# Transposing the branch inputs and merged rows on VectorE in 32x32 squares instead of on TensorE

## What is computed

```python
y_a = diff_attention(...) * silu(da_z)
y_b = mlstm(...) * silu(ml_z)
y_c = dsa_attention(...) * silu(dsa_z)
g = sigmoid(gates.reshape(b, s, 3, D_MODEL))
mixed = (g[:, :, 0] * (y_a @ w_branch[0])
         + g[:, :, 1] * (y_b @ w_branch[1])
         + g[:, :, 2] * (y_c @ w_branch[2]))
out = mixed @ w_out
x = x + rmsnorm(out, post_norm_g)
```

## Time and profile before

| | value |
|---|---|
| median of 3 runs | 1119.33 us |
| the profiled execution | 1117.77 us |
| its span in the profile | 1116.0 us |
| PE busy | 1100.3 us, 99% |
| DVE busy | 659.3 us, 59% |
| ACT busy | 540.7 us, 48% |
| POOL busy | 63.0 us, 6% |
| DMA, mean | 184 GB/s |
| mean granted clock of PE | 0.998 |

### The profile page before, as it was taken

How to read it: one execution, slowest core, us unless ns; L and a number is a source line. 1 busy time by engine, 2 the same in 40 slices (tenths; PEclk the granted TensorE clock), 3 DMA queues, 4 the chain that set the end, 5 groups by cost and what they waited for, 6 DMA issues and landing times.

```text
span 1116.0 us, 15365 instructions
## 1 busy us (share of the span) xinstructions
PE 1100.3 (99%) x5208; PEld 913.3 (82%) x5208; DVE 659.3 (59%) x928; ACT 540.7 (48%) x722; POOL 63.0 (6%) x111
## 2 busy tenths in 40 slices
PE   7999999999999999999999999999999999999997
PEld 6798888888887888889887778888888888888886
DVE  4555444665556676667866566665565545556445
ACT  4655444545555454544445444454444444435442
POOL 1000000100100011220310000000000000000000
PEclk9999999999999999999999999999999999999999
DMA  7776666565556546666656556655555466667553
GB/s 245 207 219 194 199 189 190 173 182 170 170 169 172 174 154 179 189 175 204 191 170 198 171 164 178 209 168 155 167 166 169 133 208 191 196 205 273 187 190 114
DMA packets 113514, 205.24 MB, mean 184 GB/s; under 512 B 11144, under 2 KB 17856, under 8 KB 113088
## 3 DMA queue, kind: packets, MB, share of 16 engines
q1 hardware_dynamic: 113472, 204.70, 60.5%
HBM read 202.57 MB, written 2.10 MB: 183 GB/s over the span
## 4 chain that ended last, share of the span: by engine, by line
PE 98%; DVE 1%; ACT 1%; issue 0%; DMA 0%; DVEq 0%; ACTq 0%
PE stream L1314 30%; PE stream L1316 29%; PE stream L1315 29%; PE stream L1468 2%; PE mixer L1620 1%; PE stream L1469 1%; PE mixer L1647 0%; PE mixer L1636 0%; PE mixer L1434 0%; PE mixer L1556 0%; PE mixer L1613 0%; PE mixer L1409 0%; PE mixer L1579 0%; PE mixer L1420 0%; PE mixer L1578 0%; PE mixer L1418 0%
## 5 line engine op out<-in xcount | busy, mean ns | idle before, releaser
L855 DVE TENSOR_TENSOR wlo<-raw,whi 128x1024 fp32r<-128x1024 f32 (+1 forms) x377 | 459.6, 1222 | 412.6 <-ACT whi L566 410.4
L566 ACT ACTIVATE whi<-raw 128x1024 fp32r<-128x1024 f32 (+1 forms) x377 | 397.0, 1054 | 540.0 <-PE stream L1316 509.9
L1314 PE MATMUL stream<-whi,xboth 128*128 128x512 f32 (+1 forms) x1248 | 492.5, 395 | 4.8 <-DVE wlo L855 3.3
L1316 PE MATMUL stream<-whi,xboth 128*128 128x512 f32 (+1 forms) x1248 | 484.4, 388 | 0.0
L1315 PE MATMUL stream<-wlo,xboth 128*128 128x512 f32 (+1 forms) x1248 | 483.5, 387 | 0.0
L1314 PEld LDWEIGHTS stream<-whi,xboth 128*128 128x128 f32 x1248 | 234.3, 188 | 56.3 <-issue 10.1
L1316 PEld LDWEIGHTS stream<-whi,xboth 128*128 128x128 f32 x1248 | 234.2, 188 | 48.8
L1315 PEld LDWEIGHTS stream<-wlo,xboth 128*128 128x128 f32 x1248 | 234.6, 188 | 45.4
L1314 PE MATMUL stream<-whi,yhi 128*128 128x512 f32 x192 | 76.7, 399 | 0.0
L1316 PE MATMUL stream<-whi,ylo 128*128 128x512 f32 x192 | 74.9, 390 | 0.0
L1315 PE MATMUL stream<-wlo,yhi 128*128 128x512 f32 x192 | 74.8, 389 | 0.0
(11 more groups left out here) (256 smaller groups left out, 595.3 us busy)
## 6 DMA issues: line engine op xcount, KB each, us to landing
raw<-in_w_in SPq DMA_DIRECT2D x287, 512.0 KB, 3.6
raw<-in_w_branch SPq DMA_DIRECT2D x48, 512.0 KB, 4.6
raw<-in_w_out SPq DMA_DIRECT2D x32, 512.0 KB, 4.6
raw<-in_w_in SPq DMA_DIRECT2D x10, 256.0 KB, 3.1
mixed<-in_x SPq DMA_DIRECT2D x8, 256.0 KB, 5.5
area<-in_x SPq DMA_DIRECT2D x2, 1024.0 KB, 9.3
out<-area SPq DMA_DIRECT2D x8, 256.0 KB, 2.3
raw<-in_dsa_w_uv SPq DMA_DIRECT2D x4, 256.0 KB, 2.9
```

Source lines behind the costliest of these rows:

```text
L566: nc.scalar.activation(whi[:, slot, :, 0:width], raw[:, slot, :, 0:width], ACT.Copy).then_inc(whi_ready, 1)
L855: nc.vector.tensor_tensor(wlo[:, slot, :, 0:width], raw[:, slot, :, 0:width], whi[:, slot, :, 0:width].bitcast(F32), ALU.subtract).then_in ...
L1314: nc.tensor.matmul(to, left_hi[:, kt, tokens], high, start=first, stop=False)
L1316: last = nc.tensor.matmul(to, left_lo[:, kt, tokens], high, start=False, stop=final)
```

## The change

PE no longer transposes the inputs of branches B and C, nor `mixed` columns 0 to 1535; the last 512 columns (8 blocks) stay on PE. DVE moves each 32x32 square from its quadrant of partitions to the mirrored one. One instruction takes one source quadrant and one target quadrant: 8 squares at a time for B and for `mixed`, 4 at a time for C. This makes 32 instructions for B, 64 for C and 48 for `mixed`. The results lie in SBUF (`yb_T`, `yc_T`, `merged_T`), and ACT and DVE read the high and low parts from there instead of from PSUM. The loops of DVE over the turns are written out. SP waits for `ylo_ready` 13 in place of `y_psum` 8.

```diff
+        yb_T = [view(room0, 0, 4, SEQ), view(scratch, 768, 4, SEQ)]
+        yc_T = [view(area0[:, c, :], 2048, 4, SEQ) for c in range(2)]
+        merged_T = [view(area0[:, c // 2, :], 1024 * (c % 2), 4, SEQ) for c in range(3)]
...
-            sp.wait_ge(y_psum, 8)
+            sp.wait_ge(ylo_ready, 13)
...
# ACT
-            def turn_y(n):
+            def round_y(n, turned):
                 for b in range(4):
-                    act.wait_ge(y_psum, 4 * n + b + 1)
-                    nc.scalar.activation(yhi[:, 2 * b:2 * b + 2, :], M[b][:, :].rearrange("p (k s) -> p k s", k=2),
+                    act.wait_ge(y_turned, 2 * n + b // 2 + 1)
+                    nc.scalar.activation(yhi[:, 2 * b:2 * b + 2, :], turned[b // 2][:, 2 * (b % 2):2 * (b % 2) + 2, :],
                                          ACT.Copy).then_inc(yhi_ready, 1)
             act.wait_ge(units_done, PV.unit0)
-            turn_y(0)
+            round_y(0, yb_T)
...
             act.wait_ge(units_done, PP[2].unit0)
-            turn_y(1)
+            round_y(1, yc_T)
...
-                if v >= PAIR_UNITS - 2:
-                    merged_high(2 * v - 20)
-                    merged_high(2 * v - 19)
+                if v >= PAIR_UNITS - 3:
+                    act.wait_ge(units_done, PP[2].unit(PP[2].turns - 1, FULL_UNITS))
+                    merged_high(2 * v - 18)
+                    merged_high(2 * v - 17)
...
                     if g == 0 and u == 2:
-                        for b in range(4, 8):
+                        for b in range(6, 8):
                             merged_high(b)
...
# DVE
+            def turn_block(to, of, n):
+                p, c = n // 4, n % 4
+                return nc.vector.transpose(to[c * 32:(c + 1) * 32, :, :, p * 32:(p + 1) * 32],
+                                           of[p * 32:(p + 1) * 32, :, :, c * 32:(c + 1) * 32])
...
-            with dve.Fori(0, IDX_TURNS) as i:
+            for i in range(IDX_TURNS):
                 for v in range(PAIR_UNITS):
                     split_unit(PP[0], i, v)
                     s, u = v // 3, v % 3
+                    if u < 2:
+                        turn_yb(i * 8 + 2 * s + u)
...
-            with dve.Fori(IDX_TURNS, PP[0].turns) as i:
+            for i in range(IDX_TURNS, PP[0].turns):
                 for v in range(PAIR_UNITS):
                     split_unit(PP[0], i, v)
+                    if v >= PAIR_UNITS - 4:
+                        for n in range(2):
+                            turn_yb(i * 8 + 2 * (v - (PAIR_UNITS - 4)) + n)
...
-            with dve.Fori(0, PP[1].turns) as i:
+            for i in range(PP[1].turns):
                 for v in range(PAIR_UNITS):
                     split_unit(PP[1], i, v)
+                    if i > 0 and v < 8:
+                        for n in range(2):
+                            turn_yc(i - 1, 2 * v + n)
...
                 gate_branch(PP[1], i, 4)
-            turn_y(1)
+            for n in range(16):
+                turn_yc(PP[1].turns - 1, n)
+            split_y(1, yc_T)
...
             for v in range(PAIR_UNITS):
                 split_unit(PP[2], PP[2].turns - 1, v)
-                if v >= PAIR_UNITS - 2:
-                    merged_low(2 * v - 20)
-                    merged_low(2 * v - 19)
+                if v < 8:
+                    for n in range(2):
+                        turn_mixed(2, 2 * v + n)
+                if v >= PAIR_UNITS - 3:
+                    merged_low(2 * v - 18)
+                    merged_low(2 * v - 17)
             gate_branch(PP[2], PP[2].turns - 1, 8)
...
# PE
             pe.wait_ge(idx_relu_ready, IDX_HEADS)
-            turn_y(area1)
...
-            pe.wait_ge(dsa_y, 1 + TILES * DSA_HEADS)
-            turn_y(area0)
...
-                if v == PAIR_UNITS - 3:
-                    pe.wait_ge(mixed_added, 2 * (4 + 2))
-                    for b in range(4):
-                        turn_merged(b)
...
                     if g == 0 and u == 1:
                         pe.wait_ge(mixed_added, 2 * 4 * (BRANCHES - 1))
-                        pe.wait_ge(merged_lo, 4)
-                        for b in range(4, 8):
+                        for b in range(6, 8):
                             turn_merged(b)
```

More of the change, by code:

```diff
@@ L334, in build @@
         ya_fetched, ya_psum = sem("ya_fetched"), sem("ya_psum")
[L335 removed]
+        y_turned, yhi_ready, ylo_ready = sem("y_turned"), sem("yhi_ready"), sem("ylo_ready")
         gate_tanh, prod_ready, mixed_added, iw_fetched = (sem("gate_tanh"), sem("prod_ready"), sem("mixed_added"),
@@ L1204, in _, with turn_yc @@
             steps.step(nc.vector.tensor_copy(select[0:TOPK, 0:P], causal[0:TOPK, 0:P]))
-            with dve.Fori(0, PP[1].turns) as i:
-                steps.enter(i, 2 * 4)
+            def turn_yc(i, n):
+                if n == 0:
+                    dve.wait_ge(dsa_y, 4 * i + 5)
+                columns = slice(3 * WIDTH + i * 256, 3 * WIDTH + (i + 1) * 256)
+                last = turn_block(yc_T[i // 2][:, 2 * (i % 2):2 * (i % 2) + 2, :].rearrange(
+                                      "p k (t s) -> p k t s", t=TILES),
+                                  area0[:, :, columns].rearrange("p t (k d) -> p k t d", d=P), n)
+                if n == 15 and i % 2 == 1:
+                    last.then_inc(y_turned, 1)
+            for i in range(PP[1].turns):
+                steps.enter(0, 2 * 4)
                 for v in range(PAIR_UNITS):
@@ L1235, in _, with turn_mixed @@
                 gate_branch(PP[1], i, 4)
-                steps.leave(PP[1].turns)
-            turn_y(1)
+                steps.leave(1)
+            for n in range(16):
+                turn_yc(PP[1].turns - 1, n)
+            split_y(1, yc_T)
+            def turn_mixed(c, n):
+                if n == 0:
+                    dve.wait_ge(mixed_added, 2 * (PP[1].turns + c + 1))
+                last = turn_block(merged_T[c].rearrange("p k (t s) -> p k t s", t=TILES),
+                                  mixed[:, :, c * GROUP:(c + 1) * GROUP].rearrange("p t (k d) -> p k t d", d=P), n)
+                if n == 15:
+                    last.then_inc(merged_turned, 1)
             dve.wait_ge(mixed_added, 2 * PP[1].turns)
-            with dve.Fori(0, PP[2].turns - 1) as i:
+            for i in range(PP[2].turns - 1):
                 for v in range(PAIR_UNITS):
                     split_unit(PP[2], i, v)
+                    if i > 0 and v < 8:
+                        for n in range(2):
+                            turn_mixed(i - 1, 2 * v + n)
                 gate_branch(PP[2], i, 8)
@@ L1549, in branch_units @@
                 multiply(part, i, v, v - FULL_UNITS, HALF_UNITS, (part.group0 + 1) % 2, yhi, ylo)
-            def turn_y(area):
-                for b in range(4):
-                    for j in range(2):
-                        for t in range(TILES):
-                            kt = 2 * b + j
-                            last = nc.tensor.transpose(M[b][:, j * SEQ + t * P:j * SEQ + (t + 1) * P],
-                                                       area[:, t, 3 * WIDTH + kt * P:3 * WIDTH + (kt + 1) * P],
-                                                       ident[:, :])
-                    last.then_inc(y_psum, 1)
             pe.wait_ge(banks_free, 4 + 2 * (PP[0].group0 - 1))
```

38 lines of the change are left out of this document (27 added, 11 removed).

## The result

The changed kernel takes 1124.34 us (median of five runs, 1123.74 to 1125.07) against 1119.33 for the kernel before (five runs, 1117.76 to 1120.76): a ratio of 1.0046, 95% interval 1.0033 to 1.0058. It is slower by 5.0 us where +1.6 us was forecast. In a later comparison it took 1122.89 against 1119.36 us, a ratio of 1.0027 (1.0017 to 1.0037), +3.5 us. Both intervals exclude no change. The forecast class, within 0.2%, was wrong by the first; the interval of the second reaches down to 0.17%. The forecast range, 1117.3 to 1124.5, held the time. The profiled execution of the first comparison took 1124.34 us, its span is 1122.6 us, mean granted clock 0.995.

The account below looks back on a forecast made before the run. PE was taken as the bound, busy 1100.3 of 1116.0 us. The three stage hand-overs, +0.44 + 1.32 - 0.15 = +1.6 us, moved the median from 1119.33 to 1120.9 us; range 1117.3 to 1124.5.

Parts of the forecast that it names:

- Price of a transpose: On DVE, new transposes follow each other with a gap: 0.33 us for 4 squares, 0.45 us for 8.
- Rival 1: DVE transposes overlap as same-partition instructions do, giving 1118.6 us; chance 0.10.
- Inside the turns: nothing: Between splits, 126 of 144 DVE transposes, at most two a unit (0.9 us), cost PE no wait.
- First joint, +0.44: PP[0] to PV: transposes delay DVE's products, so a 2.1 us PE wait replaces the 1.7 us saving; +0.44 us.
- Second joint, +1.32: PP[1] to PP[2]: sixteen DVE transposes delay unit 4, a 3.0 us PE wait; +1.32 us against before.
- Third joint, -0.15: PP[2] to PO: PE waits for `mixed_added`, but only eight transposes remain there, 0.87 us instead of 1.74; -0.15 us.
- Sum, +1.6: Whole kernel: the three stage hand-overs add +1.6 us, median 1120.9 us, +0.14%, called the same; chance 0.43.
- PE's busy time down by 6 us: Sign expected in the profile after: PE's busy time down by 6 us.
- rival 3: PP[1] to PP[2] decides: slower once a 4-square transpose takes 0.37 us or more, 1122.0 to 1123.5 us; chance 0.35.
- two-pass case: Turning squares on DVE takes two passes, 0.46 and 0.72 us a transpose, giving 1123.5 us; no separate chance.
- Rival 2: Waits at the stage hand-overs don't form because the ring has more lead: 6.1 us gained, 1113.2 us; chance 0.12.

Follow-up runs that it names:

- e3: The changed kernel with all merged rows transposed on PE again, B and C staying on DVE: 1122.2 us, ratio 1.0031.
- e1: The changed kernel with the input of branch B transposed on PE again: 1120.78 us, ratio 1.0008.
- e2: The changed kernel with the input of branch C transposed on PE again: 1121.27 us, ratio 1.0015.
- e8: The changed kernel with x and post_g loaded behind w_out's first loads and PE's last eight transposes after unit 3 of PO: 1118.91 us, ratio 0.9999.
- after: The changed kernel as profiled in the first comparison, against the kernel before: 1124.34 us, ratio 1.0046.
- again: The changed kernel, unaltered, run and profiled in a later batch against the kernel before: 1122.89 us, ratio 1.0027.
- e5: The changed kernel with C's last sixteen transposes writing into the quadrant they read from, so squares are misplaced: one execution of 1120.91 us.
- e6: The changed kernel with C's last sixteen transposes spread, four behind each of the first four splits of PP[2]: 1120.72 us, ratio 1.001.
- e7: The changed kernel with B's last transposes one unit earlier and the two products ahead of PP[0]'s last split: 1121.32 us, ratio 1.0016.
- e9: The changed kernel with C's transposes spread, products first, and later loads and last eight PE transposes, all together: 1112.86 us, ratio 0.9936.
- e10: The kernel before, all transposes on PE, with only the loads of x and post_g behind w_out's first loads: 1119.34 us, ratio 1.0003.

## Why the prediction was right in its terms and wrong in its class

- **Price of a transpose.** Forecast spacings 0.33 and 0.45 us; measured (5.04 - 0.30) / 15 = 0.316 and, from pairs of 0.90 with 0.436 for one, 0.46. The choice of "a gap, because the next one writes other partitions" was right, and the same-quadrant run shows that this is the reason. Rival 1 is refuted.
- **Inside the turns: nothing.** Right. No PE wait inside a turn is new, and b to c is the same within 0.2 us in all profiles.
- **First joint, +0.44.** A wait of 2.1 us was forecast, 1.93 came, released by the products as said. Without a fall a to b and b to c together give, from e3 and before, 871.19 - 870.83 = +0.36.
- **Second joint, +1.32.** The chain, link by link, as forecast; 3.0 us of wait forecast, 2.56 in the waits, 2.95 - 0.23 = 2.7 by the starts of PE's matmuls. By e1 against e2: +1.32; that it meets the forecast to the hundredth is luck, since 0.22 of it is their different wait before `PO`.
- **Third joint, -0.15.** By e2 against before: -0.15. The wait before the last eight was to be 2.2 us and is 1.9.
- **Sum, +1.6.** Without falls +1.53. That the terms agree to 0.1 us is partly luck, since e1, e2 and e3 are one execution each.
- **PE's busy time down by 6 us.** Wrong, down by 0.3: the slow matmuls of three falls took its place, 0.63 us each where they are 0.39. In e8, the changed kernel without falls, PE's busy time is 1094.5 us, down by 5.8. This line of the page was the first sign.
- **The step that failed** is the sentence behind rival 3: that the clock is at its upper level through a wait of 2.79 us, so that only the wait of 3.0 us at the second joint might bring it down. One execution in which it had stayed up was read as a bound. It is none: behind that same wait the clock fell in 4 of 13 profiles (after, again, e5, e6), behind the wait of 1.93 at the first joint in 5 of 7, behind 2.56 at the second in 3 of 6, behind 1.9 at the third in 2 of 8. With these shares the new waits cost 5/7 x 1.68 + 3/6 x 1.52 + 2/8 x 1.62 = 2.4 us more, a mean of +3.9 us, between the +3.5 and +5.0 measured. That term, which a text with two new waits of 2 and 3 us needed, was left out of the sum and only mentioned. The shares are pooled over different edits of the kernel, so the 2.4 is an estimate.
- **The range** held 1124.34 by luck. Its upper end, 1124.5, was set by the two-pass case, transposes of 0.46 and 0.72 us, which didn't come; what filled the upper part of the range is the clock, for which it had no term.
- **Rival 3** gave the right side by the wrong mechanism: its turning point, 0.37 us a transpose, wasn't reached. Its two-pass case is also summed a little high: from its own figures t4 = 0.286 + 0.123 + 0.04 = 0.45 and t8 = 0.409 + 0.246 + 0.04 = 0.70, which gives +4.0 us in place of the +4.2 behind 1123.5. **Rival 2**, that the saving stays, was put down to a ring with more lead; what it takes is to keep the joints' chains short, and then some 6.5 us are there, by the stretches (6.63) as well as by the median (6.5).

What stays open: the shares rest on few executions, and why all five executions of the first comparison had falls, and only nine of twelve in the second, isn't known. Whether a fall at the start makes one at the first joint likelier (all four profiles with the one had the other, and e2 had the second alone) wasn't tried.

## What to carry to other kernels

Work taken off the bounding engine is worth its length only where that engine can go on with something; at a hand-over between stages, list first what the next wait hangs on, and move the taken work out from ahead of it, into the slack behind splits of other units. Here the same 144 transposes on VectorE cost 3.5 to 5 us with eighteen of them ahead of what PE waits for, and gain 6.5 us with these spread out and the third joint's loads and last transposes later. A new wait of TensorE like these, 1.9 to 2.6 us, is priced twice, once as a wait and once as about 1.6 us times the chance that the clock falls behind it, even if the new wait only takes the place of work and ends no later; and one trace in which it didn't fall is not a bound. Behind shorter waits in these profiles, 1.26 us in all thirteen, 1.08 in e5 and 1.53 in e7, no fall was seen.

## What the hardware showed that was not expected

- The same wait in the same place is followed by a fall of TensorE's clock in one execution and not in the next: at J1, 1.93 us of idle time, five to two; each fall costs 1.5 to 1.7 us. The moment of the fall varies too: at J2 it comes 0.3 us before the wait's end in the changed kernel's second profile and 0.7 us behind it in e7. The Trainium skill (TensorE: Matmul & The Clock Gate, The HAM clock gate) describes the moment at which the clock first rises as varying from run to run; the traces agree, with the first rise near 12 us in e1, e9 and e10 and at 6 to 8 us in the other ten.
- It needs no wait. In the profile of e6 the clock fell at 405 us, where PE had been doing eight products of four rows of weights and four of 4x4, without idle time (start us, us, PE):

```profile
403.45 1.99 PE L1509 MATMUL mixer<-scratch,selrow 4*128 4x256 f32 x8
405.29 0.35 PE L1514 MATMUL mixer<-ident,scratch 4*128 4x4 f32 x4
405.57 0.75 PE L1382 MATMUL stream<-whi,xboth 128*128 128x512 f32 x1
406.11 0.63 PE L1383 MATMUL stream<-wlo,xboth 128*128 128x512 f32 x1
```

- Two VectorE transposes that keep their quadrants start 0.21 us apart on average (e5), two that change one 0.316 (the changed kernel), with 128 elements in each of 32 partitions.
